# One product of 512 columns in the search: rounded weights meet tokens and token remainders together

## Reference

```python
def peer_ffn(h, wq, subkeys, u, v):
    q = (hf @ wq).reshape(T, PEER_HEADS, 2, PEER_QDIM // 2)
    s = jnp.einsum('thpd,hpnd->thpn', q, subkeys)
    s1, i1 = lax.top_k(s[:, :, 0], PEER_TOPK)
    s2, i2 = lax.top_k(s[:, :, 1], PEER_TOPK)
    cand = (s1[..., :, None] + s2[..., None, :]).reshape(T, PEER_HEADS, PEER_TOPK * PEER_TOPK)
    top_s, pos = lax.top_k(cand, PEER_TOPK)
    idx = jnp.take_along_axis(cand_idx, pos, axis=-1)
    w = jax.nn.softmax(top_s, axis=-1)
    ...
        act = gelu(jnp.einsum('cd,chkd->chk', x_c, u[idx_c]))
        return jnp.einsum('chk,chkd->cd', w_c * act, v[idx_c])
```

## Time and profile before

| | us |
|---|---|
| median of 3 runs | 1612.58 (1611.77 to 1613.16) |
| profiled execution | 1611.59 |
| its span | 1609.7 |
| TensorE busy | 1503.8 (93%) |
| VectorE busy | 1179.6 (73%) |
| ScalarE busy | 820.8 (51%) |
| GpSimd busy | 19.8 (1%) |
| the search, from the first product to the last Gelu's start | 795.3 to 1004.4 |

### The profile page before, as it was taken

The page is one execution under the profiler, slowest core; times in us unless marked ns, Lnnn a source line. Parts: engine busy times, 40 slices in busy tenths (PEclk is TensorE's granted clock), DMA queues, the critical chain, the costliest instruction groups (busy, mean ns, idle before and its releaser), DMA issues.

```text
span 1609.7 us, 30083 instructions
## 1 busy us (share of the span) xinstructions
PE 1503.8 (93%) x10194; PEld 1387.9 (86%) x10194; DVE 1179.6 (73%) x2188; ACT 820.8 (51%) x1222; POOL 19.8 (1%) x25
## 2 busy tenths in 40 slices
PE   5899886999989999889999998999899999999997
PEld 5788875999869999778999998999878888889996
DVE  4667655788655566665389898989789999976665
ACT  6544555544456466635567666555433333344443
POOL 0000000000021000000000000000000000000000
PEclk9898989999999999899999999999999999999999
DMA  6443342555544532154476676434467777766553
GB/s 264 109 153 113 109 140 81 163 183 182 202 145 141 179 126 79 53 194 159 139 226 210 206 224 208 135 129 144 144 221 240 241 238 242 244 201 205 183 184 129
DMA packets 97486, 276.40 MB, mean 172 GB/s; under 512 B 10756, under 2 KB 37252, under 8 KB 96900
## 3 DMA queue, kind: packets, MB, share of 16 engines
q1 hardware_dynamic: 65808, 240.92, 45.5%
q10 hardware_dynamic: 31604, 34.49, 6.5%
HBM read 259.11 MB, written 16.25 MB: 171 GB/s over the span
## 4 chain that ended last, share of the span: by engine, by line
PE 80%; DVE 9%; ACT 5%; issue 3%; DMA 2%; ACTq 0%; DVEq 0%; SPq 0%
PE acc L1078 7%; PE acc L1081 7%; PE acc L1082 7%; PE ring L539 6%; PE ring L542 6%; PE ring L543 6%; PE acc L1000 5%; PE acc L1004 4%; PE acc L1005 4%; PE ring L1042 4%; PE acc L539 3%; PE acc L542 3%; PE acc L543 3%; DVE sb_halves L1591 2%; PE ring L1065 2%
## 5 line engine op out<-in xcount | busy, mean ns | idle before, releaser
L1591 DVE TENSOR_TENSOR sb_halves<-sb_raw,sb_halves 128x1024 fp32r<-128x1024 f32 x450 | 546.7, 1228 | 217.3 <-ACT sb_halves L1140 199.9
L1140 ACT ACTIVATE sb_halves<-sb_raw 128x1024 fp32r<-128x1024 f32 x450 | 469.8, 1057 | 382.9 <-PE acc L1078 166.7
L1000 PE MATMUL acc<-sb_XH,sb_halves 128*128 128x256 f32 x800 | 234.5, 293 | 7.7 <-DVE sb_halves L1591 7.1
L539 PE MATMUL ring<-sb_XH,sb_halves 128*128 128x256 f32 x784 | 224.2, 286 | 4.6 <-DVE sb_halves L1591 4.6
L1005 PE MATMUL acc<-sb_XH,sb_halves 128*128 128x256 f32 x800 | 226.6, 283 | 0.0
L1004 PE MATMUL acc<-sb_XL,sb_halves 128*128 128x256 f32 x800 | 226.5, 283 | 0.0
L542 PE MATMUL ring<-sb_XL,sb_halves 128*128 128x256 f32 x784 | 223.1, 285 | 0.0
L543 PE MATMUL ring<-sb_XH,sb_halves 128*128 128x256 f32 x784 | 223.0, 284 | 0.0
L1078 PE MATMUL acc<-sb_halves,sb_coefh 128*128 128x512 f32 x512 | 200.5, 392 | 6.7 <-DVE sb_coefl L2110 6.7
L1081 PE MATMUL acc<-sb_halves,sb_coefh 128*128 128x512 f32 x512 | 200.3, 391 | 0.0
L1082 PE MATMUL acc<-sb_halves,sb_coefl 128*128 128x512 f32 x512 | 199.9, 391 | 0.0
(11 more groups left out here) (333 smaller groups left out, 2546.2 us busy)
## 6 DMA issues: line engine op xcount, KB each, us to landing
sb_raw<-wstream SPq DMA_DIRECT2D x450, 512.0 KB, 3.6
ahead<-sb_early ACTq DMA_DIRECT2D x100, 128.0 KB, 2.6
sb_area<-ahead ACTq DMA_DIRECT2D x98, 128.0 KB, 3.3
sb_area<-gains ACTq DMA_DIRECT2D x4, 512.0 KB, 4.9
sb_area<-consts SPq DMA_DIRECT2D x1, 1782.0 KB, 16.7
sb_area<-mem ACTq DMA_DIRECT2D x1, 1024.0 KB, 11.6
relvec<-sb_area ACTq DMA_DIRECT2D x1, 1024.0 KB
sb_area<-keys ACTq DMA_DIRECT2D x1, 1024.0 KB, 4.7
```

The lines of the kernel that those rows point to most:

```text
L539: ins = mm(out, w[0], x[0], start=first, stop=False)
L1000: ins = mm(o, w[0], XH[:, c, :], start=c == 0, stop=False)
L1140: A(hi[:, r, :], raw[:, r, :], ACT.Copy).then_inc(S("hi_ready"), 1)
L1591: tt(lo[:, r, :], raw[:, r, :], hi[:, r, :].bitcast(F32), ALU.subtract).then_inc(S("lo_ready"), 1)
```

## The change

In the search a tile is now made by `hidden_pair`: `XH` and `XL` lie side by side as one tensor `X`, and the rounded weights meet both in one product of 512 columns that fills the whole bank; the weights' remainder meets `XH` in a product of 256 columns that adds to the bank's first half. The sum of the two halves has still to be formed. ScalarE copies the whole bank to `pair` in SBUF (`copy_pair`), GpSimd adds the halves into `early`, and ScalarE takes the Gelu there in place and stores it (`activate_sum`), one tile later than the copy. The bank is free when the copy is done. The first four tiles are written out in front of the first loop. Tiles 68 to 99 stay with `hidden_ahead` and `activate_ahead`.

```diff
-        XH = sb("XH", at, KC * T, F32R).rearrange("p (c t) -> p c t", c=KC)
-        XL = sb("XL", at + KC * T, KC * T, F32R).rearrange("p (c t) -> p c t", c=KC)
+        X = sb("X", at, 2 * KC * T, F32R).rearrange("p (s c t) -> p s c t", s=2, c=KC)
+        XH, XL = X[:, 0], X[:, 1]
...
+        pair = pl.take(2 * 2 * T).rearrange("p (b n) -> p b n", b=2)
...
+            def hidden_pair(n, k):
+                r = (E0 + k) % NR
+                pe.wait_ge(S("lo_ready"), E0 + n + 1)
+                pe.wait_ge(S("early_copied"), n + 1)
+                o = acc[:, k % 2, 0, :]
+                for c in range(KC):
+                    w = part(r, lambda z: z[:, c * P:(c + 1) * P])
+                    ins = mm(o, w[0], X[:, :, c, :], start=c == 0, stop=c == KC - 1)
+                    if c == 0:
+                        ins.then_inc(S("piece_free"), 1)
+                    ins = mm(o[:, 0:T], w[1], XH[:, c, :], start=False, stop=False, skip_group_check=True)
+                ins.then_inc(S("early_hidden"), 1)
...
             pe.nop().then_inc(S("early_gelu"), 2)
+            pe.nop().then_inc(S("early_copied"), 2)
             for t in range(NT):
                 with pe.Fori(ROUTES_AT[t - 1] // 4 if t else 0, ROUTES_AT[t] // 4) as i:
                     for k in range(4):
-                        hidden_ahead(4 * i + k, k)
+                        hidden_pair(4 * i + k, k)
...
+            def copy_pair(m, k, i):
+                n = m + 4 * i
+                act.wait_ge(S("early_hidden"), n + 1)
+                act.wait_ge(S("early_sum"), n + 1)
+                A(pair[:, k % 2, :], acc[:, k % 2, 0, :], ACT.Copy).then_inc(S("early_copied"), 1)
+
+            def activate_sum(m, k, i):
+                n = m + 4 * i
+                act.wait_ge(S("early_sum"), n + 3)
+                A(early[:, k % 2, :], early[:, k % 2, :], ACT.Gelu).then_inc(S("early_gelu"), 1)
+                act.wait_ge(S("early_gelu"), n + 3)
+                act.dma_start(ahead[bass.ds(n, 1)].rearrange("o p t -> (o p) t"), early[:, k % 2, :]
+                              ).then_inc(S(f"early_out{k % 2}"), 16)
...
             for t in range(NT + 1):
                 n0, n1 = (0, *EXP_AT)[t], (*EXP_AT, ROUTES_AT[1])[t]
+                if t == 0:
+                    for k in range(4):
+                        round_ahead(k, 0)
+                        copy_pair(k, k, 0)
+                        if k:
+                            activate_sum(k - 1, k - 1, 0)
+                    n0 = 4
                 with act.Fori(0, (n1 - n0) // 4) as i:
                     for k in range(4):
                         round_ahead(n0 + k, i)
-                        activate_ahead(n0 + k, k, i)
+                        copy_pair(n0 + k, k, i)
+                        activate_sum(n0 + k - 1, (k - 1) % 4, i)
+                if t == NT:
+                    activate_sum(n1 - 1, 3, 0)
...
+            with pool.Fori(0, ROUTES_AT[1] // 4) as i:
+                for k in range(4):
+                    pool.wait_ge(S("early_copied"), 4 * i + (k + 3))
+                    pool.wait_ge(S(f"early_out{k % 2}"), 32 * i + 16 * (k // 2 + 1))
+                    G.tensor_tensor(early[:, k % 2, :], pair[:, k % 2, 0:T], pair[:, k % 2, T:2 * T], ALU.add
+                                    ).then_inc(S("early_sum"), 1)
```

More of the change, by code:

```diff
@@ L1432, in activate_ahead @@
                               ).then_inc(S(f"early_out{k % 2}"), 16)
+            act.nop().then_inc(S("early_sum"), 2)
             for k in range(2):
```

## The result

The changed kernel takes 1626.86 us (median of 5 runs, 1622.73 to 1628.91) against 1612.58 (1611.09 to 1614.02) of the kernel before on the same chip: a ratio of 1.0087 (95% interval 1.0069 to 1.0105), 14.3 us slower. Its profiled execution took 1623.06 us with a span of 1621.3, 11.6 over the span of before. It was one of the two short ones of the five, 3.8 us under the median; what the longer ones spent more on was not profiled.

What follows compares the result with a forecast made beforehand. TensorE was taken to bound A and C, VectorE B and D, with ScalarE's iterations becoming the bound in C after the change; -3 + 3 + 7 + 2 + 2.5 = +11.5 on 1612.58 gave 1624 us, range 1613 to 1636.

Steps and rivals of the forecast that it cites:

- A: Search tiles 0 to 27, 82.3 us, bound by TensorE: at best -4.7, at worst 0, taken as -3 us.
- the term of 0.11 us per tile: TensorE's saving in the search: a tile takes 2.77 instead of 2.88 us, 7.5 us over 68 tiles if TensorE-bound throughout.
- The rival that the saving is not there: A 512-column product alternating with 256 costs two of 256; A gains 0 to -1, about 1627 us; chance 0.10.
- B: Search tiles 28 to 35, 27.9 us, bound by VectorE's wide operations: +3 us for GpSimd's adds (0 to 5).
- C: Search tiles 36 to 59: six ScalarE iterations of 13.0 us, 78.0 against 71.0, so +7.0 us.
- D: Search tiles 60 to 67, as B but with 3 us more air on VectorE: +2 us (0 to 5).
- Handover: From tile 67 to the table's products: 1.5 us more wait, half a chance of 2 for slower clock; +2.5 us.
- The rule read from the earlier trace: A ScalarE loop entered with another table than its end leaves reloads each iteration; the first loop should lose its loads.
- the first rival: Table loads stay in the first loop too: +11 us on top, about 1635 us; chance 0.10.
- the third rival: No table loads in any loop, ScalarE stays under TensorE: 0, or about 1607.5 us with cheap adds; chance 0.15.
- The slack of 0.7 us: ScalarE's true room in one four-tile search iteration of the kernel before: 10.87 us needed of 11.6.
- The second rival: VectorE against GpSimd is the bound: an add costs 1.0 us, lost for nearly each tile; about 1638 us; chance 0.10.

Runs made afterwards that it cites:

- e5: e2 with only TensorE's products of 512 and 256 columns, no copy or add, product with the tokens' remainders left out: 1600.08 us, ratio 0.9921.
- e2: The kernel before with four tiles written out ahead of each of the search's three loops, nothing else changed: 1605.30 us, ratio 0.9965.
- e3: The changed kernel without GpSimd's add; the Gelu reads the copy's first half, product with the tokens' remainders left out: 1620.63 us, ratio 1.0055.
- e1: The changed kernel with four tiles written out ahead of each of the three loops, not only the first: 1616.68 us, ratio 1.0033.
- e6: The changed kernel with ScalarE's release of the table's first product moved ahead of the search: 1624.78 us, ratio 1.0073.
- e8: e1 with ScalarE's release of the table's first product ahead of the search and four store buffers instead of two: 1609.11 us, ratio 0.9974.
- e9: e8 without GpSimd's add, product with the tokens' remainders left out: 1603.00 us, ratio 0.994.
- e4: The changed kernel with one single-column Exp between the written-out tiles and the first loop, bringing its table loads back: 1636.65 us, ratio 1.0153.
- e7: e2 with ScalarE's release of the table's first product moved ahead of the search: 1603.49 us, ratio 0.995.
- e11: e7 run again, unchanged, on the chip of e9: 1602.50 us, ratio 0.9939.

## Why the prediction came out as it did

The sign, the size and the main mechanism held: 1624 was forecast and 1626.9 measured, 2.9 more. That the spans differ by 11.6 us where the forecast's sum is +11.5 is luck: the parts sum to +14.1, and an early start of the search takes 2.4 back. By its steps, on the profiled executions:

- **A, -3 forecast, -2.6 measured.** Right in sum, by other parts. The saving on TensorE was mis-sized: the term of 0.11 us per tile measured 0.05 (chunk 0.354, not 0.346). It had priced a product of 512 columns by a stage that has nothing else, at 0.226 us; alternating with products of 256 it takes 0.236 from start to start, and the one of 256 takes 0.117. The rival that the saving is not there was half right. 28 tiles make 1.5 (e5 against e2), the loads' going 1.4 (e2), and the add takes 0.5 back (e3: 79.24 against 79.70), together 2.4 of the 2.6. The -2.6 is that of an execution in which no late store falls into A: e1 and e6, with the same code in A, have 80.9 and 82.2 us.
- **B, +3 forecast, +1.2 measured.** The add lasts 0.73 us when free (0.6 forecast). Its price depends on what else holds B up: 2.7 us where no loads are left (e8 against e9), close to the forecast, but 1.0 where they are (the changed kernel against e3). The windows of B show why: VectorE is busy for 25.8 of 28.1 us in e3 and for 28.6 of 29.1 in the changed kernel, so that most of what the adds take it would have waited for late roundings anyway. The forecast had B bound by VectorE at 27.9 us; its wide operations do run without a gap, but when they begin was set by the loads, which were worth 1.8 us in B (e2).
- **C, +7 forecast, +9.5 measured.** The iteration was right (13.14 against 13.0, 78.8 against 78.0). The other 1.6 is one add behind a store: the prediction let the add start when the copy ends, and did not follow the buffer that it writes into, whose store took 3.96 us from issue to landing here and 4.99 in e6. It falls on C by chance: e6 and e4 have 78.9 and 78.5 there with the add, e3 78.8 without it. With e8's four buffers no such wait is left, and C is 68.6 instead of e1's 70.8.
- **D, +2 forecast, +1.9 measured.** All of it is the add: e3 has 27.7.
- **Handover, +2.5 forecast, about +4.1 measured.** The wait was right (1.5 forecast, 1.46 measured). The clock's fall had half a chance at 2 us; it fell, and the third group of table products came 7.39 us behind the first instead of 4.73, 2.7 more. e6 shows that the wait brings it: with a gap of 0.53 the clock stayed. It fell at this place in all four executions with a gap of 3.03 us or more (the changed kernel, e1, e3, e4) and in none with 1.28 or less. Behind the 2.74 us from which the forecast took its half, it fell in 8 of 13.
- **The table loads.** The rule read from the earlier trace rows held, and e1, e2 and e4 show it from both sides. e4's A is the first rival's price; the third rival (no loads in any loop) is e1, forecast at 0 and measured at a ratio of 1.0033 (+5.3 us). Its four stages are 1.8 us shorter than before; what is longer is the handover, by 3.5, with the fall of the clock behind it, and a search that began 4.5 us later. The slack of 0.7 us, on the other hand, did not mean that the old kernel lost little by its loads: e2 takes 6.6 us less in the four stages without them, where some 2 were expected.
- **VectorE against GpSimd.** The second rival's bound did not come: TensorE was busy for 79.6 of A's 79.7 us. The collision on two-input operations was as forecast, at 0.4 to 0.6 us each, but it comes to few: 21 for 68 adds, not one for nearly each tile. Besides the remainders it hit sums of 256 columns in the lists (0.41 to 0.97 us), which the forecast had not counted as operations with two inputs. The Trainium skill ("SBUF — State Buffer", section "SBUF: two separate sides") says that whichever starts first, a GpSimd operation or a VectorE operation that has two SBUF inputs or runs in a 2-port performance mode, holds the shared pair for its whole instruction. The trace agrees for the wide operations and the remainders (870.57 to 874.63 above). The small operation with one tensor input was hit too (0.16 to 0.73 us); whether it ran in such a mode no trace here shows.

One thing stays open, where the search begins. Among the kernels with `X` as one tensor the search began between 792.9 and 800.4 us, among the others between 795.2 and 795.6, though nothing ahead of it was edited but where the tokens lie. Whether this comes from their place was not tried. In part it is a matter of the single execution: e5's profiled one, with the start at 800.4, took 4.5 us more than the median of its five, and that of the changed kernel, with 792.9, took 3.8 less. It blurs single totals by some us, as does the clock behind the search. So it stays open, too, why e9, whose stages are 1.9 shorter than e11's, has a median 0.5 longer.

## What to carry to other kernels

Read an engine's room from its timeline, start to start over one iteration, with table loads and the waits ahead of DMA issues; its busy share showed 60 of 80 us where it was the bound. Before work is given to an idle engine, look at what runs beside it in the stages where another engine is the bound: 0.7 us on GpSimd cost VectorE some 0.5 each time that the two met, 4.6 us in B and D together, and the adds made B and D each 2.7 us longer (e8 against e9) where the product gave 2.8 in all (e5). And take a change apart: of this one the part that paid was the four tiles written out ahead of a loop, which the old kernel could have in all three loops, for 0.35% (e2) and together with the early release for 0.5 to 0.6% (e7, e11). And look at more than one execution before a difference of 1 or 2 us in a stage is given a cause: one late store, or one fall of the clock that comes in 8 of 13 executions, is as large.

## What the runs showed of the hardware

- A loop of ScalarE over roundings and Gelus had 2 loads of 1.28 us in each iteration where it was entered behind an Exp, and none where four tiles ahead of it ended on a Gelu (e1, e4). In e1 both functions ran on one table, so the loads were no need of the loop's body.
- A gap of 3.03 us on TensorE was followed by a granted clock of 0.50 up to 1020 us, over 5 us after its end, and eight products took 2.05 instead of 1.16 us; gaps of 1.28 in the kernel before and 0.53 in e6 were followed by none. The same gap of 2.74 to 2.75 us in the table's stage was followed by 0.50 in 8 of 13 executions.
- VectorE and GpSimd took turns by whole instructions: an add that began during a wide operation ended 0.59 us after it, and the next operation of VectorE lost 0.41.
- An operation of VectorE with 8 columns and one tensor input lasted 0.73 instead of 0.16 us beside a GpSimd add; an add that takes 0.73 us alone lasted up to 2.84.
- A product of 512 columns took 0.226 us from start to start among its like and 0.236 when alternating with one of 256, which took 0.117 then and 0.120 among its like.
